# The first weight block ahead of the first quarter of x, and a small load behind the second quarter

## What is computed

```python
def reference(x, ...):
    h = x
    for layer in range(2):
        u = rmsnorm(h, norm_mix[layer])
        if layer % 2 == 0:
            h = h + even_mixer(u, w_in, ...)     # proj = u @ w_in; mLSTM heads and GLA heads; @ w_out
        else:
            h = h + s5_mixer(u, lam_re, lam_im, log_dt, ...)
        h = h + conv_ffn(rmsnorm(h, norm_ffn[layer]), ...)
    return rmsnorm(h, norm_final)

def s5_mixer(u, lam_re, lam_im, log_dt, ...):
    dt = jnp.exp(log_dt)
    lam_bar = jnp.exp(lax.complex(lam_re, lam_im) * dt)
    ...                                          # powers of lam_bar, a scan over the positions
```

## Time and profile before

| | |
|---|---|
| median of 3 runs | 2056.63 us (2056.1 to 2057.16) |
| profiled execution, own time | 2056.3 us |
| its span | 2054.3 us |
| PE busy | 2011.7 us, 98% |
| DVE busy | 1584.7 us, 77% |
| ACT busy | 1128.1 us, 55% |
| POOL busy | 569.1 us, 28% |
| moved by DMA | 398.71 MB, mean 194 GB/s |

### The profile page before, as it was taken

One profiled execution on the slowest core, in us unless ns is written; L12 is line 12 of the kernel. 1 busy time (PEld: TensorE's weight loads), 2 busy tenths in 40 slices (PEclk: granted clock), 3 DMA queues, 4 the chain that ended last, 5 costly groups with the idle time before them and its releaser, 6 DMA issues.

```text
span 2054.3 us, 40444 instructions
## 1 busy us (share of the span) xinstructions
PE 2011.7 (98%) x12944; PEld 1759.9 (86%) x12944; DVE 1584.7 (77%) x2214; ACT 1128.1 (55%) x1654; POOL 569.1 (28%) x723
## 2 busy tenths in 40 slices
PE   7999999999999999999999889999999999999997
PEld 6888888888888888888888788888888888888886
DVE  7877668888888888878888797788888888865554
ACT  6554455456666656654555435566656666544443
POOL 8999012950000000027666591100000000001110
PEclk9999999999999999999999999999999999999999
DMA  7555435556666555557777995555555555566664
GB/s 237 164 184 175 133 123 164 188 190 202 216 211 207 185 191 186 190 168 229 242 224 244 297 262 174 190 196 192 184 191 187 190 188 187 187 183 191 187 190 131
DMA packets 147446, 398.71 MB, mean 194 GB/s; under 512 B 23344, under 2 KB 48560, under 8 KB 147392
## 3 DMA queue, kind: packets, MB, share of 16 engines
q1 hardware_dynamic: 126752, 379.30, 58.3%
q10 hardware_dynamic: 20640, 18.75, 2.8%
HBM read 377.02 MB, written 18.87 MB: 193 GB/s over the span
## 4 chain that ended last, share of the span: by engine, by line
PE 86%; POOL 8%; DVE 2%; DMA 1%; ACT 1%; issue 1%; ACTq 0%; SPq 0%; DVEq 0%; POOLq 0%
PE bank L381 49%; PE bank L380 25%; PE bank L377 3%; PE bank L378 1%; PE bank L2021 1%; PE bank L2023 1%; PE bank L2022 1%; DVE lo L359 1%; POOL tab L927 1%; POOL ut L927 1%; PE bank L2051 1%; POOL nt L707 1%; POOL nt L706 0%; POOL nt L703 0%; PE bank L2228 0%
## 5 line engine op out<-in xcount | busy, mean ns | idle before, releaser
L359 DVE TENSOR_TENSOR lo<-raw,hi 128x1024 fp32r<-128x1024 f32 x698 | 889.4, 1280 | 195.5 <-ACT hi L352 182.1
L352 ACT ACTIVATE hi<-raw 128x1024 fp32r<-128x1024 f32 x698 | 734.1, 1057 | 404.1 <-PE bank L381 335.1
L381 PE MATMUL bank<-aa,hi 128*128 128x512 f32 x2558 | 894.9, 392 | 0.0
L381 PE MATMUL bank<-xx,hi 128*128 128x512 f32 x2236 | 783.9, 392 | 0.0
L380 PE MATMUL bank<-aa,lo 128*128 128x256 f32 x2558 | 715.5, 280 | 0.0
L380 PE MATMUL bank<-xx,lo 128*128 128x256 f32 x2236 | 626.5, 280 | 1.3 <-DVE lo L359 0.8
L381 PEld LDWEIGHTS bank<-aa,hi 128*128 128x128 f32 x2558 | 480.1, 188 | 101.0
L381 PEld LDWEIGHTS bank<-xx,hi 128*128 128x128 f32 x2236 | 419.5, 188 | 87.3
L380 PEld LDWEIGHTS bank<-aa,lo 128*128 128x128 f32 x2558 | 481.4, 188 | 6.3 <-DVE lo L359 0.3
L380 PEld LDWEIGHTS bank<-xx,lo 128*128 128x128 f32 x2236 | 421.1, 188 | 8.6 <-DVE lo L359 1.4
L390 ACT ACTIVATE lowt<-bank 128x256 f32<-128x256 f32 x212 | 81.2, 383 | 219.5 <-PE bank L381 212.4
(11 more groups left out here) (369 smaller groups left out, 1913.0 us busy)
## 6 DMA issues: line engine op xcount, KB each, us to landing
raw<-in_up SPq DMA_DIRECT2D x344, 512.0 KB, 3.3
raw<-in_down SPq DMA_DIRECT2D x160, 448.0 KB, 3.5
raw<-in_w_in SPq DMA_DIRECT2D x98, 512.0 KB, 3.5
raw<-in_w_out SPq DMA_DIRECT2D x32, 512.0 KB, 3.7
raw<-in_down SPq DMA_DIRECT2D x32, 512.0 KB, 4.3
raw<-in_glu SPq DMA_DIRECT2D x32, 512.0 KB, 4.2
s_c<-cp ACTq DMA_DIRECT2D x16, 256.0 KB, 3.3
s_p<-ut ACTq DMA_DIRECT2D x32, 128.0 KB, 5.5
```

Of the source, the lines that this page charges most:

```text
L352: A.activation(hi[:, s, :], raw[:, s, :], ACT.Copy).then_inc(hi_done, 1)
L359: V.tensor_tensor(lo[:, s, :], raw[:, s, :], hi[:, s, :].bitcast(f32), SUB).then_inc(lo_done, 1)
L381: last = TE.matmul(bank[:, :], hi[:, s, w], x2(k)[:, :, :], start=False, stop=k == total - 1)
```

## The change

Three places change. On SP's queue, block 0 is issued ahead of quarter 0 of x, and `lam` goes behind quarter 1. On ACT, the high half of block 0 is made ahead of the high halves of quarter 0. On DVE, the low half of block 0 is made ahead of all low halves of x, and tiles 0 to 11 of x follow in one piece ahead of block 1.

```diff
@@ -474,8 +474,6 @@
             def load_x(q):
                 sp.dma_start(h[:, 4 * q:4 * q + 4, :], t["x"][:, 4 * q:4 * q + 4, :]).then_inc(x_in[q], 16)
-            load_x(0)
-            sp.dma_start(lam[:, :, :], t["lam"]).then_inc(s5_in, 16)
@@ -526,7 +524,9 @@
             fetch(B_IN, 4, 0, 0, t["w_in"][0, :, :], BW)
+            load_x(0)
             load_x(1)
+            sp.dma_start(lam[:, :, :], t["lam"]).then_inc(s5_in, 16)
             load_x(2)
             fetch(B_IN, 4, 0, 1, t["w_in"][1, :, :], BW)
             load_x(3)
@@ -948,8 +948,8 @@
             a.wait_ge(gains_in, 16)
+            act_split(a, B_IN, 4, 0, range(1))
             x_high(0)
-            act_split(a, B_IN, 4, 0, range(1))
             x_high(1)
             x_high(2)
             act_split(a, B_IN, 4, 0, range(1, 2))
@@ -1395,9 +1395,8 @@
                 for k in range(k0, k1):
                     gain_low(v, -1, k)
-            x_low(0, 4)
             dve_split(v, B_IN, 4, 0, range(1))
-            x_low(4, 12)
+            x_low(0, 12)
             dve_split(v, B_IN, 4, 0, range(1, 2))
             x_low(12, KT)
             dve_split(v, B_IN, 4, 0, range(2, 4))
```

## The result

The changed kernel takes 2062.56 us (median of 8 runs, 2061.09 to 2064.93), the kernel before 2056.12 us in the same comparison (2055.02 to 2057.16). The ratio is 1.0031, with a 95% interval of 1.0022 to 1.004. That is 6.4 us or 0.31% slower, beyond the 2060.7 at which my range ended, and over the 0.2% that I called telling.

A forecast was written before the change was run, and what follows sets the result against it. POOL's chain from the `lam` load to the meeting point at 131.87 was taken to bound the opening: `lam` +2.9, first hold -1.0, PE's -0.4 off the path, so +1.9 on 2056.63: 2058.5 us, range 2056.0 to 2060.7.

The forecast's parts named there:

- what bounds the opening: Opening: POOL's chain from `lam` and PE's from x and block 0 meet at 131.87; PE's arrives 1.3 us earlier.
- PE's earlier start: First matmul: about 9.1, 1.4 us earlier, with 0.4 left after block 1; off the path, worth nothing.
- `x_low` doesn't hold POOL: DVE's `x_low(0, 12)` over POOL's first instructions, 9.5 to 13.8: no hold, going by the trace against the skill page.
- from 131.87 on the same work follows with the same distances: Behind the meeting point: every engine pays just the lateness of POOL's chain, with unchanged intervals afterwards.
- the clock: PE at block 1: 1.0 us idle could prolong the slow pace, PE 1.9 us late at worst; costed at nothing.
- `lam` behind quarter 2: Upper bound on `lam`'s landing: 10.7, +4.2 us; used for the range's high end, 2060.7.
- what POOL gets back: POOL's list to L728: 2.9 less 1.0 recovered, 1.9 us later; bounds +0.9 to +3.9.
- 2.9 for `lam`: SP's load queue: `lam` behind quarter 1 lands at about 9.4 instead of 6.5, 2.9 us later.
- the first hold: POOL at L656, held beside DVE's first `lo` split: this hold goes, giving back 1.0 us.
- a few instructions earlier in its list: POOL beside later DVE splits: splits keep former times within some tenths, POOL meets them slightly earlier in its list.
- the cover: PE before the meeting point: 1.3 us of wait plus POOL's 1.9, 3.2 us, hides small PE delays.
- Rival 3: POOL held through `x_low(0, 12)`, starting in earnest at 13.8: +6.2, 2062.8 us; chance 0.05.

The follow-up runs named there:

- e2: Kernel before with only the `lam` load moved behind quarter 1 of x: 2063.03 against 2056.56 us, ratio 1.0032.
- e5: Changed kernel with `lam` issued ahead of block 0, POOL's list as it was: 2056.46 against 2056.51 us, ratio 1.0001.
- e3: Changed kernel with 14 useless matmuls on PE ahead of its wait at the meeting point: 2060.5 against 2056.56 us, ratio 1.0018.
- e12: Changed kernel with `lam` one place earlier, behind quarter 0 of x: 2056.3 against 2056.78 us, ratio 1.0003.
- e8: Changed kernel with `lam` ahead of block 0, and blocks 40 and 41 split before the wait for POOL: 2056.42 against 2056.78 us, ratio 1.0.
- e4: Changed kernel with ACT and DVE splitting blocks 40 and 41 before they wait for POOL: 2060.31 against 2056.56 us, ratio 1.0019.
- e15: Changed kernel run again unaltered, as a repeat: 2061.49 against 2056.19 us, ratio 1.0025.
- e14: Changed kernel with DVE's block that waits for POOL's polynomial moved behind the next split: 2061.96 against 2056.19 us, ratio 1.0026.
- e13: Changed kernel with `lam` one place later, behind quarter 2 of x: 2062.9 against 2056.78 us, ratio 1.0032.

## Why the prediction was wrong

*Right: what bounds the opening.* Two chains meet at 131.87, and what counts is POOL's, which begins with `lam`. e2 shows it with one moved line. PE's earlier start was worth nothing, as e5 shows. `x_low` doesn't hold POOL: L651 to L657 run beside it without a long step.

*Wrong, the step that failed: "from 131.87 on the same work follows with the same distances".* I let PE's wait grow to 3 or 4 us and took it for lateness alone. It was 4.2 us, and behind it the clock fell: 14 matmuls took 5.9 us, 2.8 us in all. I had weighed the clock, but only at the first tile, where the idle time is 1.4 us and the pace of 0.12 us from before it was there again behind it. e3 gives its price as some 2.5 us: 3.9 over before with the wait filled, 6.4 without (5.3 in the repeat). By the traces it is 2.8 us in the changed kernel, 2.3 in its repeat and 2.7 in e2. Of the 4.5 us between forecast (+1.9) and result (+6.4) it is the larger part, and this term alone carries the time from inside the range (3.5 us over before, 2060) to outside of it. (The high end of the range, 2060.7, is itself a little short: 2056.63 and the 4.2 of `lam` behind quarter 2 are 2060.8.)

*Wrong: what POOL gets back.* The sum had 2.9 for `lam` and -1.0 for the first hold. `lam` was 2.45 us later. The first hold was saved (e12 shows it clean), but the list behind it got longer by more: 121.8 us instead of 120.7, so +1.1 where I had -1.0. The 3.54 us by which L728 ended late lie within the bounds that I gave to it, +0.9 to +3.9, and near the end that I thought the less likely. That is 1.6 us more than the 1.9 of the sum. I let POOL meet the same splits "a few instructions earlier in its list". DVE's splits did fall within a microsecond of their former times, but by 100 us POOL's list lay one round of DVE behind, and got some of that back only when DVE paused.

*Of no effect: the first microseconds.* First matmul at 8.56 (forecast 9.1), wait for block 1 of 1.4 us (1.0), DVE's wait for the polynomial 0.9 us (0.5), a wait of 1.4 us on PE behind it. At the end of the first tile PE was 1.2 us earlier than before and not 0.4, since the slow pace ended at 11.9, ahead of the wait for block 1; at 113 us it was 0.6 late. All of it lay under the cover, as said.

*Rival 3 had the number by accident.* Its 2062.8 is what was measured, by a mechanism that isn't there: POOL's first instruction wasn't held past 11.7, it had done five by then.

## What to carry to other kernels

When a change makes an engine wait longer, ask what the wait does to the engine and not only when it ends: a PE that idles for 4 us may come back at half its pace, and the loss is then nearly twice the lateness. A load of 96 KB can be the head of the longest chain though its consumer is needed 120 us later; follow the chain to its first transfer before a load is called small. A chain of many small POOL instructions beside DVE's large ones has no fixed length: it took from 117.0 (e8) to 123.5 us (e4) here. Its place moved in whole rounds of DVE and not with its start, so price a shift of it in such rounds, and see whether DVE pauses ahead of the point where it is needed.

## What was not expected of the hardware

In the same first place of the queue, block 0 was there for ACT at 4.7 us, while quarter 0 of x, as large, had been there at 6.22. I have no cause for it. A 4.2 us wait brought the half clock in all four profiles that had it at 135 us, but not for the same time: about 6 us in the changed kernel and in e2, 5.3 in the repeat (e15), and 3.4 in e14. A wait of 3.0 us brought it in e4 and not in e13. POOL's list, beside DVE's splits, took one of three places, 5.5 us apart, in all profiles but one. And extra matmuls in a wait made the kernel faster.
